# Rebuilding the expert stage of a two-block transformer kernel: split weights, static slots, and the copy of the down product on another engine

## What is computed

```python
def hier_moe(h, rg_w, rg_b, re_w, re_b, w_gate, w_up, w_down):
    """h (N,D): top-1 expert group, then top-2 experts inside it; gate = p_group * renormalised p_expert."""
    ...
    y = jnp.zeros_like(h)
    for e in range(N_EXPERTS):
        he = jax.nn.silu(h @ w_gate[e]) * (h @ w_up[e])
        y = y + comb[:, e:e + 1] * (he @ w_down[e])
    return y
```

## Time and profile before

| what | value |
| --- | --- |
| median of three runs | 3032.42 us |
| span of the profiled execution | 3032.6 us |
| PE busy | 2690.8 us (89%) |
| DVE, ACT, POOL busy | 1069.4, 795.4, 803.2 us |
| first gate or up matmul of the expert stage | 578.2 us |
| end of its last down product | 994.3 us |
| first matmul of the second block's turns | 1028.3 us |

### The profile page before, as it was taken

How to read it: one execution, slowest core, us unless ns; L and a number is a source line. 1 busy time by engine, 2 the same in 40 slices (tenths; PEclk the granted TensorE clock), 3 DMA queues, 4 the chain that set the end, 5 groups by cost and what they waited for, 6 DMA issues and landing times.

```text
span 3032.6 us, 29962 instructions
## 1 busy us (share of the span) xinstructions
PE 2690.8 (89%) x11350; PEld 2001.2 (66%) x11350; DVE 1069.4 (35%) x1664; ACT 795.4 (26%) x1438; POOL 803.2 (26%) x337
## 2 busy tenths in 40 slices
PE   6997987499999499999999579999888899899997
PEld 4675666233333379887889557888765666688886
DVE  3294453221211323332342434242312435342423
ACT  2333322000000323334333323222222323332222
POOL 2331122211212032223222313444422110134443
PEclk9898787699999799999999579999978878699999
DMA  4421022488888221121211312323221100123331
GB/s 142 135 69 42 28 92 84 167 296 300 302 279 293 86 84 56 56 70 56 70 56 56 113 42 83 97 89 92 83 64 56 54 30 14 34 81 94 97 97 69
DMA packets 277015, 311.82 MB, mean 103 GB/s; under 512 B 24752, under 2 KB 215824, under 8 KB 276912
## 3 DMA queue, kind: packets, MB, share of 16 engines
q1 hardware_dynamic: 262736, 297.65, 29.9%
q0 software_dynamic: 7648, 12.70, 1.2%
q10 hardware_dynamic: 6528, 0.03, 0.1%
HBM read 298.68 MB, written 22.66 MB: 106 GB/s over the span
## 4 chain that ended last, share of the span: by engine, by line
issue 53%; PE 16%; POOL 11%; DVE 1%; ACT 0%; DMA 0%; POOLq 0%; SPq 0%; DVEq 0%; ACTq 0%
POOL w_low L2327 10%; PE bank L1004 9%; PE bank L1017 4%; PE bank L985 1%; PE bank L1129 1%; PE bank L1107 0%; PE bank L664 0%; PE bank L666 0%; PE bank L665 0%; PE bank L990 0%; POOL og L2409 0%; DMA xg<-d_rows,gather_rows 0%; PE bank L1116 0%; DVE xn L1762 0%; PE bank L698 0%
## 5 line engine op out<-in xcount | busy, mean ns | idle before, releaser
L2327 POOL TENSOR_TENSOR w_low<-raw,w_high 128x2048 fp32r<-128x2048 f32 x149 | 683.7, 4590 | 1750.1 <-ACT w_high L1328 1750.1
L664 PE MATMUL bank<-h_high,w_high 128*128 128x512 f32 x1120 | 453.1, 405 | 17.6 <-DVE h_low L1742 7.8
L665 PE MATMUL bank<-h_low,w_high 128*128 128x512 f32 x1120 | 446.0, 398 | 0.0
L666 PE MATMUL bank<-h_high,w_low 128*128 128x512 f32 x1120 | 444.7, 397 | 0.0
L664 PE MATMUL bank<-w_high,h_high 128*128 128x512 f32 (+1 forms) x832 | 345.7, 416 | 29.8 <-POOL w_low L2327 25.6
L1328 ACT ACTIVATE w_high<-raw 128x2048 fp32r<-128x2048 f32 x149 | 284.5, 1910 | 330.7 <-PE bank L666 330.4
L665 PE MATMUL bank<-w_low,h_high 128*128 128x512 f32 (+1 forms) x832 | 331.6, 399 | 0.0
L666 PE MATMUL bank<-w_high,h_low 128*128 128x512 f32 (+1 forms) x832 | 330.8, 398 | 0.0
L1004 PE MATMUL bank<-m_w,xt 128*64 128x512 f32 x576 | 264.0, 601 | 0.0
L664 PEld LDWEIGHTS bank<-h_high,w_high 128*128 128x128 f32 x1120 | 216.8, 194 | 69.5 <-DVE h_low L1742 10.3
L666 PEld LDWEIGHTS bank<-h_high,w_low 128*128 128x128 f32 x1120 | 216.3, 193 | 46.7
(11 more groups left out here) (297 smaller groups left out, 3201.1 us busy)
## 6 DMA issues: line engine op xcount, KB each, us to landing
raw<-in_ffn_w_gu SPq DMA_DIRECT2D x88, 512.0 KB, 4.5
m_w<-in_w_gate SPq DMA_DIRECT2D x74, 512.0 KB, 5.5
m_w<-in_w_up SPq DMA_DIRECT2D x74, 512.0 KB, 6.3
raw<-in_a_w_in SPq DMA_DIRECT2D x72, 512.0 KB, 4.6
m_w<-in_w_down SPq DMA_DIRECT2D x36, 1024.0 KB, 8.5
raw<-in_ffn_w_down SPq DMA_DIRECT2D x40, 512.0 KB, 4.6
raw<-in_w_in SPq DMA_DIRECT2D x34, 512.0 KB, 4.4
raw<-in_b_w_in SPq DMA_DIRECT2D x24, 512.0 KB, 4.5
```

The source lines that it names most:

```text
L664: pe.matmul(out, sta[0], mov[0], start=start, stop=False)
L665: pe.matmul(out, sta[0], mov[1], start=False, stop=False)
L666: return pe.matmul(out, sta[1], mov[0], start=False, stop=stop)
L2327: pool.tensor_tensor(out=w_low[:, slot, :], in0=raw[:, slot, :], in1=w_high[:, slot, :].bitcast(F32), op=ALU.subtract).then_inc(low_done, 1)
```

## The change

1. **Products.** Gate and up weights are no longer read by PE as plain fp32. ACT rounds each to fp32r (`up_high`), DVE subtracts to get the rest (`up_low`), 2048 columns an instruction, four instructions a slot. The rows of a slot are split too: ACT writes their high part, DVE the low part, side by side as 128 stationary columns. PE multiplies them by `up_high` and then by `up_low`, 16 fp32r matmuls. The lower 64 rows of the product are copied out by ACT (`lower`) and added by DVE (`gated`), before the silu. `down` stays as it is.
2. **Weight runs.** Gate and up weights are loaded as one transfer each, with runs of 8 KB to a partition (row `p * 8 + k` instead of `k * 128 + p`); the norm ahead of the router writes its columns in that order.
3. **Static slots.** Slots 0 to 31 are the first 64 rows of experts 0 to 31; further slots follow. There are 32 + 4 = 36. The weights of slots 0 to 2 are loaded, and those of 0 and 1 split in part, before the router ends. The list of rows comes from a matmul of one-hot matrices (`row_hot`, `slot_hot`) and stays on the chip.
4. **Copy of the down product.** ACT does it (`out`), between the silu and the next weights.
5. **Memory.** The split weights lie where `w_high`, `w_low`, `h_high` and `h_low` are. So B_DIL is loaded but not split ahead of the stage, and B_DIL + 1 is loaded behind `y_in`; ACT and POOL split both after the stage.

```diff
@@ SP
+        def gate(ring, e, done):
+            sp.dma_start(ring[:, 0, :].rearrange("p (k n) -> p k n", k=KD), expert("w_gate", e, KD)).then_inc(done, 16)
...
+        def next_up(j, b):
+
+            e = slot_of(j)
+            sp.wait_ge(m_low, 2 * j - 3)
+            gate(w_ring[b], e, m_up[b][0])
+            sp.wait_ge(m_low, 2 * j - 2)
+            up(w_ring[b], e, m_up[b][1])
+
+        def next_down(j, b):
+            e = slot_of(j)
+            sp.wait_ge(m_down, j - 1)
+            down(w_ring[b], e, m_dn[b])
...
+            next_down(2 * i - 1, 1)
+            next_up(2 * i + 1, 1)
...
+        load_wide(B_DIL + 1, a["a_w_in_2"][0], 4, 0)
@@ PE
+            pe.wait_ge(m_high, 2 * j + 2)
+            for k in range(KD):
+                if k == KD - 1 and before is not None:
+                    pe.wait_ge(m_he, before + 1)
+                pe.matmul(G[b][:, :], xt[:, b, k, :], up_high[:, b, k, :], start=(k == 0), stop=False)
+            if before is not None:
+                turn_he()
+            pe.wait_ge(m_low, 2 * j + 2)
+            for k in range(KD):
+                last = pe.matmul(G[b][:, :], xt[:, b, k, :], up_low[:, b, k, :], start=False, stop=(k == KD - 1))
@@ ACT
+        def gate(j, b):
+
             act.wait_ge(m_gu, j + 1)
...
+            act.activation(lower[:, :], G[b][R:2 * R, :], ACT.Copy).then_inc(m_lower, 1)
+            act.wait_ge(m_gated, 2 * j + 1)
+            act.activation(sg[:, :], gated[:, 0:FE], ACT.Silu).then_inc(m_silu, 1)
...
+        def out(j, b, i):
+            act.wait_ge(m_down, j + 1)
+            if not isinstance(i, int) or i:
+                act.wait_ge(m_scat[b], 16 * i)
+            for half in range(2):
+                last = act.activation(y_out[:, b, 512 * half:512 * half + 512], G[2 + half][0:R, :], ACT.Copy)
+            last.then_inc(m_y, 1)
+
+        def period(j, b, uses, i=None):
+
+            gate(j - 1, 1 - b)
+            if i is not None:
+                out(j - 2, b, i)
+            up_next(j + 1, 1 - b, uses, 0)
+            rows_high(j + 1, 1 - b)
+            turned_he(j - 1)
+            up_next(j + 1, 1 - b, uses, 1)
...
+        split_high(B_DIL, B_DIL % 2, B_DIL // 2 + 1)
+        split_high(B_DIL + 1, (B_DIL + 1) % 2, (B_DIL + 1) // 2 + 1)
@@ DVE
+        def up_part(ring, b, q):
+            dve.tensor_tensor(out=up_low[:, b, :, FE * q:FE * q + FE],
+                              in0=ring[:, q, :].rearrange("p (k n) -> p k n", k=KD),
+                              in1=up_high[:, b, :, FE * q:FE * q + FE].bitcast(F32),
+                              op=ALU.subtract).then_inc(m_low, 1)
...
+        def period(j, b):
+            inner(j - 1, 1 - b)
+            up_next(j + 1, 1 - b, 0)
+            rows(j + 1, 1 - b)
+            up_next(j + 1, 1 - b, 1)
@@ POOL
+        split_low(B_DIL, B_DIL % 2)
+        split_low(B_DIL + 1, (B_DIL + 1) % 2)
```

More of the change, by code:

```diff
@@ L180, in two_blocks_kernel @@
[L180 to L200, removed]
+    g_wide = at("g_wide", 93, [P, D])
+    rt_raw = at("rt_raw", AR + 76, [P, KD, 36])
+    rt_split = at("rt_split", AR + 77.25, [P, KD, 72], F32R)
@@ L971, in _ @@
         last.then_inc(rt_cum, 1)
+        pe.wait_ge(rt_hot, 1)
+        for c in range(2 * NT):
+            last = pe.matmul(SB[0][0:R, 0:SLOTS], row_hot[:, c, :], slot_hot[:, c, :], start=(c == 0), stop=(c == 2 * NT - 1))
+        last.then_inc(rt_list, 1)
         phase_end(5)
@@ L1041, in _ @@
         down(2 * n_trips - 1, 1, n_trips)
-        for q in range(2):
-            pe.wait_ge(m_up[0][q], 32 * n_trips + 32)
-            last = pe.matmul(SB[1][0:R, 0:R], ident[:, 0:R], m_w[:, 0, q, 0:R], start=True, stop=True)
         phase_end(6)
@@ L1497, in _, with rows_ahead @@
         phase_mark()
-        def rows_ahead(n0, out, free, r):
+        def rows_ahead(n0, out, free, r, more=True):
             for half in range(2):
                 half_read()
-                ahead(n0 + 2 * half)
+                if more or half == 0:
+                    ahead(n0 + 2 * half)
                 if half == 0:
@@ new lines, in _ @@
+        act.drain().then_inc(m_y, 1)
+        rows_high(0, 0)
+        rows_high(1, 1)
+        period(1, 1, 1)
+        period(2, 0, 2, 0)
+        period(3, 1, 2, 0)
+        with act.Fori(2, n_less) as i:
+            period(2 * i, 0, i + 1, i - 1)
+            period(2 * i + 1, 1, i + 1, i - 1)
+        period(2 * n_less2 + 2, 0, n_less2 + 2, n_less2)
+        gate(2 * n_less2 + 2, 0)
+        turned_he(2 * n_less2 + 2)
+        out(2 * n_less2 + 1, 1, n_less2)
+        gate(2 * n_less2 + 3, 1)
@@ L2024, in _ @@
         step(sub(starts, ends, ntile[:, :]))
-        begin, cut = rv[:, 0:2, :], rv[:, 3:5, :]
+        slots = cst[:, C_SLOT:C_SLOT + NE]
+        step(dve.scalar_tensor_tensor(out=starts, in0=starts, scalar=float(NE - 1), in1=slots,
+                                      op0=ALU.add, op1=ALU.subtract))
+        over, cut, own = rv[:, 0:2, :], rv[:, 3:5, :], rv[:, 6:8, :]
         for k in range(2):
@@ L2097, in _ @@
[L2097 to L2098 removed]
+        period(1, 1)
+        with dve.Fori(1, n_less) as i:
+            period(2 * i, 0)
+            period(2 * i + 1, 1)
+        period(2 * n_less2 + 2, 0)
+        inner(2 * n_less2 + 2, 0)
+        inner(2 * n_less2 + 3, 1)
+        dve.wait_ge(m_y, 2 * n_trips + 1)
         for b in range(2):
```

341 lines of the change are left out of this document (194 added, 147 removed).

## The result

The changed kernel takes 3096.45 us (median of four runs, 3093.42 to 3099.49), the kernel before 3031.65 us on the same chip. The ratio is 1.0207, with a 95% interval of 1.0192 to 1.0222: 2% slower. The profiled execution has a span of 3097.7 us, 65.1 us above that of before.

What follows compares the result with a forecast made beforehand. PE bounds the old stage at 11.49 us a slot; afterwards the port-delayed gather loop does, at 14.4. 35 x (14.4 - 11.49) = +102, -14 ahead, +9 behind: +97 on 3032.6, 3130 us; range 2980 to 3190 (8 in 10).

Steps and rivals of the forecast that it cites:

- B: Rival: POOL's transfer gets the ports between DVE's two subtractions, gather issued at 6.7, period 12.4 us, 3060 us; chance 0.20.
- A: Likeliest case: shared ports delay the gather past both DVE subtractions; period 14.0 to 16.1 us, 3108 to 3190; chance 0.42.
- period T: Time per slot in the rebuilt stage, end of one `down` to the next: 14.4 us, against 11.49 before.
- The gather loop becomes the bound: Rebuilt stage: no engine needs more than 8.5 us a slot, so the loop through `y_out`, scatter and gather sets the period.
- The ports delay POOL: Gather in each slot: DVE's two-input subtractions and POOL exclude each other, so the issue moves from 4.4 to 8.7 us.
- The landing: Gathered rows, from issue to arrival: 3.8 us, between the earlier minimum 3.4 and median 4.8.
- The end of `down`: PE's work after the wait for the rows: half of `down`, four matmuls of 0.428 plus 0.17, 1.9 us.
- The clock: PE after idling: at 0.50 the half `down` takes 3.4 instead of 1.7 us, period 16.1; upper bound, not taken.
- Ahead of the stage: Before the first product: list and `rt_split` changes bring the gather 8 us earlier, 2 more to the product; together -14.
- Behind it: After the stage: B_DIL + 1 lands late, its rounding and POOL's `w_low` delay the norms; +9.2, bounds 0 to +12.
- C: Rival: ports cause no delay in the gather loop; period 11.1 us, 3014, or 10.2 and 2982; chance 0.20.
- D: Rival: the gather is early enough altogether, DMA or PE bounds; period 8.4 to 9.4 us, 2919 to 2954; chance 0.13.

Runs made afterwards that it cites:

- e1: Changed kernel with POOL issuing the gather of slot j + 2 ahead of the scatter of slot j - 2 instead of behind it: 2938.61 us, ratio 0.9676.
- e2: Kernel before the change, with the gather put ahead of the scatter in the same way: 3035.86 us, ratio 1.0005.
- e5: Changed kernel with gate and up weights loaded in eight transfers each, runs of 1 KB instead of 8 KB: 3093.03 us, ratio 1.0187.
- e8: Changed kernel with only half of the gate and up weights loaded, all other work keeping its size: 3038.88 us, ratio 1.0014.
- e3: Changed kernel with one of the eight `up_low` matmuls per slot, seven left out: 3107.88 us, ratio 1.0242.
- e7: Changed kernel with ACT's rounding of B_DIL + 1 behind the norms' squares instead of ahead of them: 3089.94 us, ratio 1.0180.

## Why the prediction came out as it did

The forecast was 3130 us, slower by 97; it is 3096, slower by 65. The direction and the place were right. The time lies between the ranges of B (3045 to 3094) and A (3108 to 3190), in neither, and the size is the sum of several misses that partly cancel. Term by term, in us after the end of a `down` (measured: means over 31 slots in the middle of the stage):

| | forecast | measured |
| --- | --- | --- |
| the gather's transfer begins | 8.7 | 6.08 |
| its landing takes | 3.8 | 6.06 |
| from there to the end of `down` | 1.9 | 1.57 |
| period T | 14.4 | 13.71 |

**The gather loop becomes the bound: right.** e1 (-158 us) shows it, and e2 shows that it wasn't the bound before. No engine is full in the stage, as the sums of 8.3, 6.9 and 6.5 us a slot said: 177.45 and 172.65 us over the 27 to 28 slots of the window are 6.4 for ACT and 6.2 for DVE. PE's 294.02 are 10.6, more than 8.3, since part of its work ran at the lower clock.

**The ports delay POOL: right in kind, wrong in the count.** The index copy is held by the first subtraction as stepped (2.09 against 0.20, and 0.50 with short pieces). The step that failed is "The gather is issued at 8.7 instead of 4.4". In 19 of 28 slots POOL's transfer got in ahead of the second subtraction, as in rival B (6.0 us after `down` in the slot shown). In the other 9 it was held as in A, to about 8.9 us after `down`, and even there the rows landed no later. I had seen that 0.3 us decide this. A subtraction that begins during a transfer is not held by it, against the reading that whichever begins first keeps the other out, as a slot of the changed kernel shows (timeline):

```profile
703.63 0.96 POOL L2487 DMA_INDIRECT xg<-d_rows,gather_rows  x1 [0.77 <-POOL gather_rows L2485]
...
704.11 2.29 DVE L2115 TENSOR_TENSOR up_low<-w_ring,up_high 128x2048 fp32r<-128x2048 f32 x1 [0.69 <-ACT up_high L1571]
```

**The landing: wrong.** "Landing I take as 3.8 ... since the queues carry only 3.38 MB in a longer period" failed. The mean load fell (295 to 247 GB/s), but the load at the moment of the gather rose. In the earlier trace rows the landing was 4.8; now it is 5.9 in the median and 7.8 in the slot shown. I had read SP's order in the diff, `next_down` ahead of `next_up`, only as a count of bytes, not as times. Before, the gate and up weights went out ahead of the end of the `down` (701.79), and only the down weights behind it (SP's queue, the slot of the earlier trace rows):

```profile
698.53 0.37 SPq L557 DMA_DIRECT2D m_w<-in_w_gate  x1
...
700.50 0.37 SPq L558 DMA_DIRECT2D m_w<-in_w_up  x1
701.96 0.38 SPq L564 DMA_DIRECT2D m_w<-in_w_down  x1
```

The gather followed at 706.25. The new order ties all three matrices to the end of `down`, the same event that releases the gather. The last paragraph of the prediction named long runs as the way a landing could be stretched; e5 shows that it is not the runs, e8 that it is the bytes under way. The early issue and the late landing cancel by luck: 6.1 + 6.1 instead of 8.7 + 3.8, so that the rows land 12.1 us after `down` where 12.5 were forecast.

**The end of `down`: wrong.** "The other half of `down` is four matmuls of 0.428 and the last one's end of 0.17, 1.9 us" counts two matmuls too many. The wait stands ahead of the last two, which take 1.02 us in every slot of the kernel before. With that term T would have been 13.5 and the forecast about 3099. It would have been near for a wrong reason, since the issue and the landing cancel. For the same reason the loop before had more slack than the 0.3 us stated: the sum of 11.2 comes down to 10.3, 1.2 us below 11.49. The term "35 x (14.4 - 11.49) = +102" measured +69.4. That is a mean of 13.87 over the stage; the kernel before has 11.89 as the same mean, since both count the ends of the stage too.

**The clock.** The end of `down` takes 1.07 us in some slots and 1.97 in others, so the lower clock of the earlier trace rows is met in a part of the slots. I had taken it in none. It adds 0.9 us where it is met, not the 1.7 of the forecast's upper bound, which again counted four matmuls; over the stage it adds 14.9 us of the +69.4. e3 fits: less work on PE, a lower clock, 11 us slower (the intervals just touch).

**Ahead of the stage:** -9.1 for -14. The first gather's copy comes at 559.49 instead of 566.77, 7.3 us earlier. The forecast had 8 from the list and 3 to 4 from `rt_split`, some 11.5 together:

```profile
559.49 0.18 POOL L2485 COPY gather_rows<-slot_rows 64x1 int32<-64x1 int32 x1 [76.17 <-DVE slot_rows L2177]
```

The list itself gave more than forecast: from `cum` to that copy it is 24.4 us before and 15.1 now. The miss lies ahead of `cum`, which is copied at 544.35, 2.0 us later than before. `rt_split` takes 0.46 us, as expected. But the norm that writes with a stride takes 1.96 us a tile where it had 1.28, 2.7 us over four tiles. I had put 0 for it, and 1.3 at most. And the last sum ahead of the norms already comes 3.4 us later (488.46 for 485.05), for which no run shows a cause. In the other traces of the rebuilt kernel the first gate or up matmul comes between 567.0 and 572.6, so a few us of this term are not explained by any step.

**Behind it:** +10.3 for +9, by the mechanism named (e7). POOL's `w_low` runs from 1076.94 to 1081.45, and the norm's scaling beside it has 2.88 us instead of 1.28, as forecast. The second block is 5.5 us shorter in the ledger (1998.8 for 2004.3), but with the same code there the other traces of the rebuilt kernel have 1996.7 to 2006.3. So this is no gain that can be told from none.

**The rivals.** B described the issue of most slots, but its time of 3060 rested on the same landing of 3.8. C asked for no hold by the ports and D for an early gather; neither is what the trace has, though e1 turns the kernel into D, 2938.61 us against D's 2919 to 2954. The Trainium skill's figure of about 358 GB/s ("DMA: Bandwidth & Descriptors", Specifications), by which a slot's transfers would take an estimated 9.4 us, lies below e1's window of 374 GB/s; the measurement decides.

## What to carry to other kernels

When a bound engine is made faster, write out the loops that pass through other engines and queues, and see how near they are to the old period. Here one had 1.2 us of slack, and moving one instruction ahead of another (the gather ahead of the scatter) decided what the whole rebuild was worth: it turned 2% slower into 3.2% faster. Read from the code where in its work an engine waits; "half way" for "ahead of the last quarter" cost the forecast 30 us.

Price a small transfer by what is under way at the moment of its issue, not by the mean load. Look also for a stretch in which the queues stand empty because the next burst waits for what the last one held up. When two waits stand side by side, each experiment on one of them shows little; take both away before you call either harmless.

## What the hardware showed that I had not expected

- With seven matmuls a slot fewer on PE the kernel was 11 us slower (the intervals just touch), with the mean granted clock of the stage at 0.74 instead of 0.83.
- A gather's indirect transfer that starts inside a DVE subtraction with two SBUF inputs has a record of 2.82 us instead of 0.95; one that starts 0.5 us ahead of the subtraction has 0.96, and the subtraction its usual 2.29.
- The rows of one gather, 0.23 MB with the scattered ones, landed with the last of 3 MB of weights, about 12 us after `down`, whether issued 3.2 or 6.4 us after it. Their landing had the same median of 5.9 us with runs of 1 KB as with runs of 8 KB.
